# The last of four stages rewritten as one program, with rows kept on chip and weights loaded a stage earlier

## The chip, the cores and the metric

The kernel runs on one core of a Trainium2 chip, as one launch. The time is device microseconds (us) from the start of the program to its end; lower is better. Five engines of the core run their own instruction lists and meet through semaphores: TensorE (PE in the rows) multiplies matrices and transposes, VectorE (DVE) and ScalarE (ACT) do elementwise work and read PSUM, the memory that TensorE writes to; GpSimd (POOL) does small elementwise work, and SyncE (SP) only starts transfers here.

## The reference

Four layers run one after the other over 512 tokens of width 1024 in float32. The first three (attention with two softmaxes, attention in a neighbourhood, a gated delta rule) are not changed. The third leaves a residual stream `h` of 528 rows, 16 of them meta tokens. The fourth, cut to what matters:

```python
def shared_latent_kv(x, pos, g_norm, w_down, g_latent, w_uk, w_uv, k_gain):
    bsz, lp, _ = x.shape
    h = rms_norm_2(x, g_norm)
    c = h @ w_down
    c_kv = rms_norm_2(c[..., :KV_RANK], g_latent)
    k_pe = jnp.broadcast_to(c[..., None, KV_RANK:], (bsz, lp, MLA_HEADS, QK_ROPE))
    k_nope = (c_kv @ w_uk).reshape(bsz, lp, MLA_HEADS, QK_NOPE)
    v = (c_kv @ w_uv).reshape(bsz, lp, MLA_HEADS, V_HEAD)
    k = rms_norm_2(jnp.concatenate([k_nope, k_pe], -1), k_gain)
    k = jnp.concatenate([k[..., :QK_NOPE], rope(k[..., QK_NOPE:], pos)], -1)
    return k, v
...
def mla_layer(x, pos, k, v, g_norm, w_in, g_q_latent, w_uq, q_gain, w_out):
    bsz, lp, _ = x.shape
    h = rms_norm_2(x, g_norm)
    z = h @ w_in
    c_q = rms_norm_2(z[..., :Q_RANK], g_q_latent)
    gate = z[..., Q_RANK:]
    q = rms_norm_2((c_q @ w_uq).reshape(bsz, lp, MLA_HEADS, QK_DIM), q_gain)
    q = jnp.concatenate([q[..., :QK_NOPE], rope(q[..., QK_NOPE:], pos)], -1)
    o = chunk_causal_attention(q, k, v).reshape(bsz, lp, MLA_VW) * jax.nn.silu(gate)
    return x + o @ w_out
```

There are 8 heads; a query or key has 128 plain columns and 64 rotary ones, the rotary part of a key is the same for all heads, the latent of keys and values has 256 columns, that of queries 384, and the gate 1024.

## The kernel before

`program` (L3672) runs four stages. Tokens come in chunks: chunk 0 has the 16 meta rows, chunks 1 to 4 have 128 rows each. The third stage, `delta_layer` (L2910), ends with the output projection of its layer: TensorE (L2506), VectorE's add to the residual rows `d_rows` (L2860), and SyncE's store of each piece to `h3` in HBM (L2313). SyncE then waits until all stores have landed (L2314), and a barrier between blocks (L2915) holds all engines until it has.

The fourth stage is three functions, each a block of its own with a barrier behind it. Within a block each engine's order is the order of the code; a `Stages` object counts the named steps of an engine, and others wait for a name.

`latent_keys` (L2998): SyncE loads chunk after chunk of `h3` into two buffers in `m_tmp` (L3042), and between the second and the third chunk the gain columns, the identity, the rotary tables and `w_down` (L3046 to L3053), then the weights for keys and values (L3055) and for the query latent (L3057). For each chunk ScalarE squares and sums the row (L3081), GpSimd makes the reciprocal root (L3119, L3121), VectorE scales (L3162, one buffer `xn`), TensorE transposes 8 blocks (L3230), and VectorE (L3166) and then ScalarE (L3072) evacuate with the gains of keys and of queries. TensorE waits for all nine constants before its first transpose. Down projection `c` (L3251), its norm, its transposes (L3241). Then chunk by chunk: products for keys and values (L3269, 8 matmuls of 512 columns), squares (L3105), sums (L3203), root (L3136 to L3140), scaling (L3207), gain (L3211), rotary part (L3213), transposes (L3283, L3289), copies (L3098, L3196). The products of chunk t+1 stand ahead of the transposes of chunk t, and wait for the scaling of chunk t, since both use one pair of PSUM banks.

`latent_queries` (L3293): query latents (L3427), eight gate tiles (L3446, 8 matmuls of 512 columns each, tanh on ScalarE L3340, two steps on VectorE L3387 and L3389), then for each of four chunks of queries 9 matmuls of 512 columns (L3469), squares (L3349), sums (L3401), root (L3365, L3367), scaling (L3404), gain (L3408), rotary part (L3413 to L3417), transposes (L3481, L3486) and copies (L3345, L3395).

`latent_attention` (L3490): VectorE zeroes half of the two rotary buffers (L3597, L3599), ScalarE copies one half (L3572), and only then TensorE makes the first scores (L3525); 32 units of a head and a chunk, then the output projection (L3566), the add (L3625) and the stores.

A float32 matmul is two records in the trace (8 matmuls are x16), a transpose is one.

## Time and profile before

| | us |
|---|---|
| median of 3 runs | 3225.17 |
| lowest and highest | 3225.07, 3231.73 |
| the profiled execution, time | 3222.18 |
| its span | 3220.4 |

The profile is one execution, and its span begins and ends with the work on the engines; 1.8 us of the time lie around it. A row of the timeline gives start, duration, engine, line, what is written and read, and in brackets how long the engine had been idle and who ended that. A row of stretches gives the bounds and the length, then busy time with the number of instructions in brackets for PE, PEld (weight loads), DVE, ACT and POOL, then PEclk, the busy share of the DMA engines, and GB/s. A group of matmuls is shown some 0.16 us longer than it holds TensorE, because its last one is still draining when the next group starts; from one start to the next is the better length. The granted clock (PEclk) is a share of full speed: 1.00 is 2.4 GHz and 0.50 is 1.2 GHz.

### The profile page before, as it was taken

The page shows a single profiled execution, that of the slowest core. Times are in us where ns is not written, and L with a number is a line of the kernel's source. Part 1 is how long each engine was busy: PE and PEld are TensorE (multiplying, and loading weights), DVE is VectorE, ACT ScalarE, POOL GpSimd, SP SyncE. Part 2 cuts the span into 40 slices and gives each one's busy share as a digit, 9 for nine tenths or more (in the row PEclk, how much of TensorE's full clock was granted, in tenths as well). Part 3 has the DMA queues.
Part 4 walks back from the last instruction along what each step waited for, and adds up shares of the span by engine and source line. Part 5 has one row for each costly group of instructions (what it writes and reads, how often), then busy time and mean ns, then how long its engine had stood idle before and what let it go on. Part 6 is the DMA issues. An engine that isn't in the chain of part 4 may idle for free. (4 is left out here: it accounts for less than half of the span.)

```text
span 3220.4 us, 37627 instructions
## 1 busy us (share of the span) xinstructions
PE 3026.0 (94%) x14339; PEld 1959.2 (61%) x14339; DVE 1522.1 (47%) x3450; ACT 812.0 (25%) x2062; POOL 444.0 (14%) x745
## 2 busy tenths in 40 slices
PE   5999999999999997999999999979999999589699
PEld 2445555555555544887878786547888885244374
DVE  2344554554554435556556654334565563331431
ACT  1013333333333322123232332212122221120141
POOL 1221231231230010202011110000011110010000
PEclk8999999999999998999999999989999999799799
DMA  7330010010014004211212123042111100311001
GB/s 236 144 118 27 27 53 26 27 53 27 27 53 131 1 0 144 69 48 53 73 47 73 40 72 138 1 115 53 27 27 39 41 27 1 124 53 56 26 1 53
DMA packets 137899, 189.06 MB, mean 59 GB/s; under 512 B 21836, under 2 KB 90476, under 8 KB 135668
## 3 DMA queue, kind: packets, MB, share of 16 engines
q1 hardware_dynamic: 136520, 186.57, 18.2%
q8 instruction: 115, 1.88, 0.2%
q14 instruction: 64, 0.52, 0.1%
q10 hardware_dynamic: 1200, 0.09, 0.0%
HBM read 176.97 MB, written 9.67 MB: 58 GB/s over the span
## 5 line engine op out<-in xcount | busy, mean ns | idle before, releaser
L488 PE MATMUL a_psP<-a_w,a_uT 128*128 128x512 f32 x1536 | 700.1, 601 | 5.8 <-DMA a_w<-a_w_in 5.8
L488 PEld LDWEIGHTS a_psP<-a_w,a_uT 128*128 128x128 f32 x1536 | 280.5, 192 | 323.2 <-issue 323.2
L737 DVE TENSOR_REDUCE a_small<-a_psS 128x1 f32<-128x768 f32 (+1 forms) x192 | 140.8, 775 | 402.0 <-PE a_psS L516 402.0
L1460 PE MATMUL b_psP<-b_w,b_uT 128*128 128x256 f32 x768 | 183.8, 382 | 0.8 <-DVE b_raw L1743 0.3
L643 ACT ACTIVATE a_e<-a_psS,a_small 128x768 f32<-128x768 f32 (+1 forms) x192 | 143.8, 753 | 139.1 <-DVE a_small L737 138.7
L1460 PEld LDWEIGHTS b_psP<-b_w,b_uT 128*128 128x128 f32 x768 | 141.7, 190 | 23.7 <-issue 3.8
L1780 DVE TENSOR_REDUCE b_small<-b_psS 128x2 f32<-128x512 f32 x64 | 44.3, 691 | 213.0 <-PE b_psS L1517 213.0
L538 PEld LDWEIGHTS a_psO<-a_v,a_pT 128*128 128x128 f32 x896 | 115.1, 192 | 45.9 <-issue 45.9
L650 ACT COPY a_pT<-a_psS 128x768 f32<-128x768 f32 (+1 forms) x96 | 63.0, 656 | 311.4 <-PE a_psS L525 311.4
L1617 ACT ACTIVATE b_e<-b_psS,b_small 128x512 f32<-128x512 f32 x128 | 86.7, 682 | 192.0 <-DVE b_small L1793 190.1
L1624 ACT COPY b_e<-b_psS 128x512 f32<-128x512 f32 x128 | 71.8, 587 | 228.5 <-PE b_psS L1527 147.2
L2333 PE MATMUL d_ps<-d_uT,f_place 128*128 128x264 f32 x512 | 120.4, 388 | 6.4 <-DVE d_yT L2704 4.3
L1460 PE MATMUL b_psP<-b_wt,b_us 128*128 128x256 f32 x512 | 122.5, 387 | 4.1 <-DVE b_wt L1690 4.1
L2333 PE MATMUL d_ps<-d_uT,d_w 128*128 128x264 f32 x512 | 121.7, 392 | 4.8 <-DVE d_yT L2704 4.3
L516 PE MATMUL a_psS<-a_kT,a_qT 64*128 64x256 f32 (+1 forms) x640 | 122.4, 493 | 0.0
L538 PE MATMUL a_psO<-a_v,a_pT 128*128 128x128 f32 x896 | 115.5, 275 | 0.0
L1460 PEld LDWEIGHTS b_psP<-b_wt,b_us 128*128 128x128 f32 x512 | 96.1, 192 | 22.4 <-issue 6.6
L2333 PEld LDWEIGHTS d_ps<-d_uT,f_place 128*128 128x128 f32 x512 | 94.8, 190 | 24.2 <-DVE d_yT L2704 5.3
L2333 PEld LDWEIGHTS d_ps<-d_uT,d_w 128*128 128x128 f32 x512 | 95.9, 192 | 21.6 <-DVE d_yT L2704 5.3
L713 POOL TENSOR_TENSOR a_small<-a_small,a_eps_sum 128x1 f32<-128x1 f32 x96 | 18.2, 190 | 650.5 <-ACT a_dump L654 650.5
L800 DVE TENSOR_TENSOR a_work<-a_work 128x256 f32<-128x256 f32 x96 | 86.4, 939 | 0.4
L654 ACT ACTIVATE a_dump<-a_psO,a_small 128x128 f32<-128x128 f32 x96 | 35.3, 367 | 203.4 <-PE a_psO L538 203.4
(479 smaller groups left out, 5368.1 us busy)
## 6 DMA issues: line engine op xcount, KB each, us to landing
a_w<-a_w_in SPq DMA_DIRECT2D x16, 2048.0 KB, 8.7
b_w<-b_w_in SPq DMA_DIRECT2D x48, 512.0 KB, 3.8
a_yT<-mod_w SPq DMA_DIRECT2D x8, 1536.0 KB, 8.5
a_yT<-mod_w SPq DMA_DIRECT2D x8, 1024.0 KB, 18.2
b_yT<-b_w_in SPq DMA_DIRECT2D x16, 512.0 KB, 3.7
f_place<-bias_table SPq DMA_DIRECT2D x64, 128.0 KB
f_place<-a_w_in SPq DMA_DIRECT2D x16, 512.0 KB, 6.5
d_w<-a_w_in SPq DMA_DIRECT2D x16, 512.0 KB, 6.9
```

Source lines behind the costliest of these rows:

```text
L488: ins = nc.tensor.matmul(s.psP[:, x % 2, :], s.uT[:, a, t * P:(t + 1) * P], w[:, a, :], start=(a == 0), stop=(a == KD - 1))
L516: ins = nc.tensor.matmul(self.score_banks(k, keys)[:, a:b], s.qT[rows, h, t * P:(t + 1) * P], s.kT[rows, g % 2, h, keys.start + a:keys.sta ...
L538: ins = nc.tensor.matmul(s.psO[:, 0:P], s.pT[:, k * P:(k + 1) * P], s.v[:, g % 2, keys.start // P + k, h * P:(h + 1) * P], start=(k == 0), ...
L643: nc.scalar.activation(s.e[:, k, 0:n], self.score_banks(k, keys), ACT.Exp, bias=self.nm[i % 2][:, k:k + 1], accum_out=self.r[i % 4][:, k:k ...
L650: nc.scalar.copy(s.pT[:, 0:n], self.score_banks(0, keys)).then_inc(self.wTr, 1)
L737: nc.vector.tensor_reduce(self.nm[i % 2][:, k:k + 1], self.score_banks(k, keys), AX_X, ALU.max, negate=True).then_inc(self.mx, 1)
L800: nc.vector.tensor_tensor(r5[:, :, :, half, :], x5[:, :, :, 1 - half, :], sin, ALU.mult).then_inc(self.sined, 1)
L1460: ins = nc.tensor.matmul(out, lhsT, rhs, start=(a == 0), stop=(a == 3))
L1617: nc.scalar.activation(s.e[:, k, :].rearrange("p (b r c) -> p r b c", b=8, c=8), s.psS[:, k, :].rearrange("p (r b c) -> p r b c", b=8, c=8 ...
L1624: nc.scalar.copy(s.e[:, k, :], s.psS[:, k, :]).then_inc(self.wTr, 1)
L1780: nc.vector.tensor_reduce(self.m_ctx, ctx, mybir.AxisListType.XY, ALU.max).then_inc(self.cm, 1)
L2333: ins = nc.tensor.matmul(ps[:, 4, 0:n], s.w[h % 2][:, b, i, :], s.uT[:, b, half * n:(half + 1) * n], start=(b == 0), stop=(b == KD - 1))
```

## The change

The third stage's residual rows move to a buffer that lives through both stages (`Later.rows`, `g_rows`), and stage four reads them there. Weights and gain columns for keys are loaded by SyncE at the start of the third stage, behind its own loads (`Later.load`). The wait for the last stores moves out of the third stage to the first use that needs it (the first gate tile). The three functions of stage four become `LatentMixer` and `LatentAttention` in one block. Their PSUM banks are dealt so that keys (banks 0 to 3), queries (4 to 6) and gates (7) go side by side. The multiplication of keys and of the main part of queries by their gains moves into ScalarE's copies as a per-column scale; VectorE keeps the gain of the 64 rotary columns of queries. Two `xn` buffers take the place of one, and evacuation of a transposed chunk is split in halves between VectorE and ScalarE.

```diff
--- before.py
+++ after.py
@@ third stage
-        self.rows = sb("d_rows", [P, CH, D], F32)
+        self.rows = later.rows
...
         load_head(sp, s.w[1], a["a_w_in_2"][0], 1, self.w_in)
+        self.ahead(sp)
...
             sp.dma_start(self.h3[r, cols], s.rows[0:chunk_len(t), t, cols]).then_inc(self.stored, 16)
-        sp.wait_ge(self.stored, 16 * len(self.rest))
@@ loads at the start of the third stage
+    def load(self, sp, a, col_in, down_in, up_in):
+        g = self.gcol
+        for dst, src in ((g[:, 0:8], a["kv_norm_2"]), (g[:, 8:16], a["b_norm_2"][0]), (g[:, 16:18], a["kv_latent_norm_2"]),
+                         (g[:, 18:21], a["b_q_latent_norm_2"][0]), (g[:, 21:22], a["k_gain_2"][0:P]),
+                         (g[:, 22:23], a["b_q_gain_2"][0][0:P])):
+            sp.dma_start(dst, src.rearrange("(a p) -> p a", p=P), allow_slow_non_contiguous=True).then_inc(col_in, 16)
+        sp.dma_start(self.w_down[:, :].rearrange("p (a n) -> p a n", a=KD),
+                     a["kv_w_down_2"].rearrange("(a p) n -> p a n", p=P)).then_inc(down_in, 16)
+        w_u = self.w_u[:, :].rearrange("p (r a n) -> p r a n", r=2, a=2)
+        for r, name in enumerate(("kv_w_uk_2", "kv_w_uv_2")):
+            sp.dma_start(w_u[:, r], a[name].rearrange("(a p) n -> p a n", p=P)).then_inc(up_in, 16)
@@ LatentMixer, SyncE
+        sp.dma_start(s.w_cq, rows(W[:, 0:Q_RANK])).then_inc(self.cq_in, 16)
+        sp.dma_start(s.cos[:, :, :], a["rope2_cos"].rearrange("(t p) d -> p t d", p=P)).then_inc(self.rope_in, 16)
+        sp.dma_start(s.sin[:, :, :], a["rope2_sin"].rearrange("(t p) d -> p t d", p=P)).then_inc(self.rope_in, 16)
+        sp.dma_start(s.gain[:, 0, :], a["k_gain_2"][P:].partition_broadcast(P)).then_inc(self.rope_in, 16)
+        sp.dma_start(s.gain[:, 1, :], a["b_q_gain_2"][0][P:].partition_broadcast(P)).then_inc(self.rope_in, 16)
+        sp.dma_start(s.w_g[0], rows(W[:, Q_RANK:Q_RANK + BANK])).then_inc(self.g_in[0], 16)
+        sp.dma_start(s.w_uq, rows(a["b_w_uq_2"][0])).then_inc(self.uq_in, 16)
+        sp.wait_ge(te.sem, te.at("c%d" % LT))
+        sp.dma_start(s.w_g[1], rows(W[:, Q_RANK + BANK:Q_RANK + 2 * BANK])).then_inc(self.g_in[1], 16)
@@ LatentMixer, TensorE: the order, and the waits of a round
+        def gate(i):
...
+            elif i == 6:
+                aw("qT%d" % (LT - 1))
+            elif i == 7:
+                vw("sg5")
+            else:
+                vw("sg%d" % (i - 1))
...
+        def keys_values(t):
...
+            if t:
+                vw("kn%d" % (t - 1))
...
+                    if t and (r, j) == (0, 0):
+                        vw("kpT%d" % (t - 1))
...
+        def keys_T(t):
+            n = chunk_len(t)
+            vw("kp%d" % t)
...
+        def queries(t):
+            if t:
+                aw("qT%d" % (t - 1))
+                vw("qpT%d" % (t - 1))
...
+        for r in range(LT):
+            keys_values(r + 1)
+            gate(r + 1)
+            queries_T(r)
+            if r == LT - 1:
+                gate(5)
+            keys_T(r + 1)
+            if r < LT - 1:
+                queries(r + 1)
+        gate(6)
+        gate(7)
@@ LatentMixer, VectorE: a round
+        for r in range(LT):
+            key_sums(r + 1)
+            keys(r + 1)
+            gate(r + 1)
+            copy_qpT(r)
+            if r == LT - 1:
+                gate(5)
+            copy_kpT(r + 1)
+            if r < LT - 1:
+                query_sums(r + 1)
+                query_rest(r + 1)
+        gate(6)
+        gate(7)
@@ LatentAttention, VectorE: ahead of the first scores
+        dve.wait_ge(te.sem, te.at("kT%d" % LT))
+        nc.vector.memset(self.qp[1][0:64], 0.0).then_inc(self.qp_zero, 1)
+        dve.wait_ge(self.qp_odd, 1)
+        nc.vector.memset(s.qpT[64:128], 0.0).then_inc(self.qp_zero, 1)
@@ program
-                latent_keys(nc, sem, s, a, h3)
-                latent_queries(nc, sem, s, a)
-                latent_attention(nc, sem, s, a, h3, a["out"])
+                latent_layer(nc, sem, s, a, h3, a["out"], rows_stored, *ahead)
```

The order of TensorE in the queries of before, from the last gates to the third chunk of queries (`m_w2` and the gate weights print alike as `m_w`; L3469 are the query products, L3481 and L3486 their transposes):

```order
L3446 MATMUL m_ps<-m_w,m_ubT 128x512 x32
L3469 MATMUL m_ps<-m_w,m_cT 128x512 x18
L3481 MATMUL m_ps<-f_identity,m_tmp 128x128 x8
L3486 MATMUL m_ps<-f_identity,m_rot 128x128 x4
L3469 MATMUL m_ps<-m_w,m_cT 128x512 x9
L3481 MATMUL m_ps<-f_identity,m_tmp 128x128 x8
L3486 MATMUL m_ps<-f_identity,m_rot 128x128 x4
L3469 MATMUL m_ps<-m_w,m_cT 128x512 x9
```

The order of TensorE in one round of after (the products of keys and values L3202, one gate L3183, transposes of queries L3236 and L3240, of keys L3210 and L3214, products of queries L3229):

```order
L3202 MATMUL m_ps<-g_w_up,m_cT 128x512 x8
L3183 MATMUL m_ps<-f_place,m_ubT 128x512 x8
L3236 MATMUL m_ps<-f_identity,m_tmp 128x128 x8
L3240 MATMUL m_ps<-f_identity,g_rows 128x128 x4
L3210 MATMUL m_ps<-f_identity,m_tmp 128x128 x4
L3214 MATMUL m_ps<-f_identity,m_tmp 128x128 x8
L3229 MATMUL m_ps<-m_w,m_cqT 128x512 x9
```

Key products and a gate now stand between the products of a chunk of queries and its transposes, where before there were the products of the next chunk only, and two barriers lay between keys, queries and scores.

VectorE in the queries of before, one chunk (sums, scaling, copy of the chunk before, gain over 1536 columns, four rotary steps):

```order
L3401 TENSOR_REDUCE m_tiny<-m_tmp 128x8
L3404 TENSOR_TENSOR m_tmp<-m_ps,m_tiny 128x1536
L3395 COPY m_qpT<-m_ps 128x4x128
L3408 TENSOR_TENSOR m_tmp<-m_tmp,m_gain 128x1536
L3413 TENSOR_TENSOR m_rot<-m_tmp,m_sin 128x8x32
L3414 TENSOR_TENSOR m_rot<-m_tmp,m_sin 128x8x32
L3415 TENSOR_TENSOR m_rot<-m_tmp,m_cos 128x512
L3417 TENSOR_TENSOR m_rot<-m_rot 128x512
```

VectorE in a round of after, from the scaling of a chunk of queries on:

```order
L3518 TENSOR_TENSOR m_tmp<-m_ps,m_tiny 128x1536
L3520 TENSOR_TENSOR m_tmp<-m_tmp,m_gain 128x8x64
L3526 TENSOR_TENSOR g_rows<-m_tmp,m_sin 128x8x32
L3527 TENSOR_TENSOR g_rows<-m_tmp,m_sin 128x8x32
L3528 TENSOR_TENSOR g_rows<-m_tmp,m_cos 128x512
L3530 TENSOR_TENSOR g_rows<-g_rows 128x512
L3493 TENSOR_REDUCE m_tiny<-m_tmp 128x8
L3500 TENSOR_TENSOR m_tmp<-m_ps,m_tiny 128x1024
L3503 TENSOR_TENSOR m_tmp<-m_kpe,m_tiny 128x512
L3485 TENSOR_SCALAR g_w_down<-g_w_down 128x512
L3487 TENSOR_TENSOR g_rows<-g_w_down,m_ps 128x512
L3534 COPY g_w_down<-m_ps 128x4x128
```

The gain of queries is 512 columns (L3520) instead of 1536, the gain of keys is gone, and the sums and the scaling of keys (L3493, L3500, L3503) stand behind the whole of the queries' part and ahead of the gate (L3485, L3487) and of the copy (L3534).

SyncE at the start of the third stage of after, behind the first heads' weights (the last row is the third stage's own next load):

```order
L2239 DMA d_w<-a_w_in 128x8x128 x4
L2979 DMA g_columns<-kv_norm 128x8x1
L2979 DMA g_columns<-b_norm 128x8x1
L2979 DMA g_columns<-kv_latent_norm 128x2x1
L2979 DMA g_columns<-b_q_latent_norm 128x3x1
L2979 DMA g_columns<-k_gain 128x1
L2979 DMA g_columns<-b_q_gain 128x1
L2980 DMA g_w_down<-kv_w_down 128x8x320
L2984 DMA g_w_up<-kv_w_uk 128x2x1024
L2984 DMA g_w_up<-kv_w_uv 128x2x1024
L2239 DMA f_place<-a_w_in 128x8x128 x4
```

Nine loads, 3.3 MB, are new there; in before they stand in stage four, between the second and the third chunk of rows and behind the last chunk.

## Rows read from the trace of the kernel before

**Rows 1.** Timeline of the border between stages three and four, all engines.

```profile
2777.58 0.69 DVE L2860 TENSOR_TENSOR d_rows<-d_rows,d_ps 128x512 f32<-128x512 f32 x1 [1.03 <-PE d_ps L2506]
...
2780.78 0.07 DVE L3154 MEMSET m_half<- 128x8 f32 x1 [2.51 <-PEq L2915]
...
2782.67 1.05 ACT L3081 ACTIVATE m_v<-m_tmp 16x1024 f32<-16x1024 f32 x1 [36.89 <-DMA m_tmp<-h]
...
2784.80 0.74 DVE L3162 TENSOR_SCALAR m_tmp<-m_tmp,m_tiny 16x1024 f32<-16x1024 f32 x1 [3.59 <-POOL m_tiny L3121]
...
2794.64 1.03 PE L3230 MATMUL m_ps<-f_identity,m_tmp 16*128 16x16 f32 x8 [17.10 <-DMA m_sin<-rope_sin]
```

**Rows 2.** Busy time of each engine, granted clock and DMA in three stretches.

```profile
2778.00:2795.00 17.00, 0.35 (x4) 0.36 (x4) 1.41 (x5) 2.29 (x4) 1.46 (x4) 0.62 0.65 158
2795.00:2814.00 19.00, 8.28 (x39) 6.84 (x38) 10.34 (x36) 9.73 (x30) 2.21 (x6) 0.50 0.75 271
...
2981.00:3052.00 71.00, 43.06 (x121) 21.17 (x119) 36.05 (x36) 12.13 (x10) 7.36 (x8) 0.80 0.08 30
```

**Rows 3.** Timeline of TensorE: down projection, key transposes, query latents, gates, queries.

```profile
2828.88 4.47 PE L3251 MATMUL m_ps<-f_place,m_ukT 128*128 128x320 f32 x16
...
2867.98 1.04 PE L3283 MATMUL m_ps<-f_identity,m_tmp 128*128 128x128 f32 x8
2868.86 0.60 PE L3289 MATMUL m_ps<-f_identity,m_tmp 128*128 128x128 f32 x4
...
2895.44 20.88 PE L3427 MATMUL m_ps<-m_w,m_ubT 128*128 128x384 f32 x64 [1.05 <-PEq L3035]
...
2953.38 27.63 PE L3446 MATMUL m_ps<-m_w,m_ubT 128*128 128x512 f32 x64
2980.85 15.61 PE L3469 MATMUL m_ps<-m_w,m_cT 128*128 128x512 f32 x36
```

**Rows 4.** Timeline of one chunk of keys: squares, sums, scaling.

```profile
2864.75 1.02 ACT L3105 ACTIVATE m_tmp<-m_ps 128x1024 f32<-128x1024 f32 x1 [5.01 <-PE m_ps L3269]
...
2865.81 1.22 DVE L3203 TENSOR_REDUCE m_tiny<-m_tmp 128x8 f32<-128x1024 f32 x1 [3.00 <-ACT m_tmp L3105]
...
2869.34 1.22 DVE L3207 TENSOR_TENSOR m_tmp<-m_ps,m_tiny 128x1024 f32<-128x1024 f32 x1 [2.31 <-POOL m_tiny L3140]
```

**Rows 5.** Timeline of one chunk of queries: squares, sums, scaling, last rotary step.

```profile
2988.77 1.45 ACT L3349 ACTIVATE m_tmp<-m_ps 128x1536 f32<-128x1536 f32 x1 [7.13 <-PE m_ps L3469]
...
2990.26 1.75 DVE L3401 TENSOR_REDUCE m_tiny<-m_tmp 128x8 f32<-128x1536 f32 x1 [7.43 <-ACT m_tmp L3349]
...
2994.05 1.76 DVE L3404 TENSOR_TENSOR m_tmp<-m_ps,m_tiny 128x1536 f32<-128x1536 f32 x1 [2.04 <-POOL m_tiny L3367]
...
2999.03 0.69 DVE L3417 TENSOR_TENSOR m_rot<-m_rot 128x512 f32<-128x512 f32 x1
```

**Rows 6.** Timeline of one gate: tanh, then the product with it.

```profile
2974.18 0.60 ACT L3340 ACTIVATE m_rot<-m_ps 128x512 f32<-128x512 f32 x1 [6.27 <-PE m_ps L3446]
...
2975.27 0.69 DVE L3389 TENSOR_TENSOR m_sg<-m_rot,m_ps 128x512 f32<-128x512 f32 x1
```

**Rows 7.** Timeline ahead of the first scores.

```profile
3047.88 1.76 DVE L3597 MEMSET m_tmp<- 64x2048 f32 x1 [0.77 <-PEq L3316]
3050.13 1.76 DVE L3599 MEMSET m_qpT<- 64x2048 f32 x1 [0.48 <-issue]
...
3052.04 0.58 PE L3525 MATMUL m_ps<-m_kT,m_qT 128*128 128x16 f32 x2 [5.66 <-DVE m_qpT L3599]
```

**Rows 8.** Timeline of TensorE at the third stage's start, transposes only.

```profile
2149.11 3.68 PE L2067 MATMUL d_ps<-f_identity,d_cq 128*128 128x128 f32 x16 [1.12 <-DVE d_cq L2140]
2152.97 1.52 PE L2067 MATMUL d_ps<-f_identity,d_cq 128*128 128x128 f32 x8 [0.18 <-DVE d_cq L2140]
```

**Rows 9.** Timeline of SyncE: its first loads behind the third stage's start.

```profile
2197.62 4.18 SPq L2238 DMA_DIRECT2D f_place<-a_w_in  x4
```

**Rows 10.** Transfers of stage four: one load, its size and time from issue to landing.

```profile
m_w<-b_w_in SPq DMA_DIRECT2D x1, 1536.0 KB, 11.4
```

More of the change, by code:

```diff
@@ L2940, in _ @@
             mixer.vector(dve)
+    return mixer.stored, 16 * len(mixer.rest)
 def delta_masks():
@@ new lines, in __init__ @@
+        self.w_down = later.w_down[:, :].rearrange("p (a n) -> p a n", a=KD)
+        self.w_u = later.w_u[:, :].rearrange("p (r a n) -> p r a n", r=2, a=2)
+        self.w_cq = self.kT[:, :, :].rearrange("p h n -> p (h n)")[:, 0:KD * Q_RANK].rearrange("p (a n) -> p a n", a=KD)
+        self.w_uq = self.w2[:, :].rearrange("p (a n) -> p a n", a=3)
+        flat = self.ukT[:, :, :].rearrange("p a n -> p (a n)")[:, 0:KD * BANK]
+        self.w_g = [x.rearrange("p (a n) -> p a n", a=KD) for x in (front.place[:, :], flat)]
@@ new lines, in gate, with key_sums @@
+        def gate(i):
+            n, t = self.gates[i]
+            if i == 0:
+                dve.wait_ge(*self.rows_stored)
+            aw("tanh%d" % i)
+            ve.done(nc.vector.tensor_scalar(s.th, s.th, 0.5, 0.5, ALU.mult, ALU.add), "th%d" % i)
+            me("th%d" % i)
+            ve.done(nc.vector.tensor_tensor(s.sg[:, t, n * BANK:(n + 1) * BANK], s.th, ps[:, self.gate_bank(i), :], ALU.mult),
+                    "sg%d" % i)
+        def key_sums(t):
+            n = chunk_len(t)
+            aw("sqk%d" % t)
+            ve.done(nc.vector.reduce_sum(self.kss[t % 2][0:n], heads(s.tmp[0:n, 0, 0:D], P), AX_X), "ssk%d" % t)
@@ new lines, in copy_qpT @@
+        def copy_qpT(t):
+            tw("qpT%d" % t)
+            ve.done(nc.vector.tensor_copy(s.qpT[:, :, self.tok(t)], heads(ps[:, 6, :], P)), "qpT%d" % t)
+        nc.vector.memset(s.half[:, :], -0.5)
+        nc.vector.memset(s.kpe[:, 0], 0.0)
+        ve.done(nc.vector.memset(s.eps[:, :], EPS), "memsets")
+        normed(0)
+        normed(1)
+        scale_uk(0)
+        normed(2)
+        scale_uk(1)
+        normed(3)
+        scale_uk(2)
+        latent(0)
+        normed(4)
+        scale_uk(3)
@@ new lines, in vector @@
+        latent(1)
+        scale_uk(4)
+        for t in range(3):
+            scale_c(t)
+            latent(t + 2)
+        scale_c(3)
+        query_latent(0)
+        scale_c(4)
+        query_latent(1)
+        key_rotation()
+        query_latent(2)
+        query_latent(3)
+        for t in range(3):
+            scale_cq(t)
+        gate(0)
+        key_sums(0)
+        scale_cq(3)
+        keys(0)
+        query_sums(0)
+        copy_kpT(0)
+        query_rest(0)
+        for r in range(LT):
+            key_sums(r + 1)
+            keys(r + 1)
+            gate(r + 1)
+            copy_qpT(r)
+            if r == LT - 1:
+                gate(5)
+            copy_kpT(r + 1)
+            if r < LT - 1:
+                query_sums(r + 1)
+                query_rest(r + 1)
@@ L3328, in _ @@
+            attention.sync(sp)
+        @block.tensor
+        def _(pe):
+            mixer.tensor(pe)
+            attention.tensor(pe)
         @block.scalar
         def _(act):
[L3330 to L3335 removed]
@@ L3336, in _ @@
-            for i in range(2 * LT):
-                act.wait_ge(te.sem, te.at("z%d" % i))
-                if i >= 2:
-                    act.wait_ge(ve.sem, ve.at("sg%d" % (i - 2)))
-                ac.done(nc.scalar.activation(s.rot[:, i % 2, :], s.ps[:, 6 + i % 2, :], ACT.Tanh, scale=0.5), "tanh%d" % i)
-            def copy_q(t):
-                act.wait_ge(te.sem, te.at("qT%d" % t))
-                ps = s.ps[:, 4 * (t % 2):4 * (t % 2) + 2, :].rearrange("p b n -> p (b n)")
-                ac.done(nc.scalar.copy(s.qT[:, :, tok(t)], heads(ps, P)), "qT%d" % t)
@@ L3347, in _ @@
[L3347 to L3352 removed]
+            mixer.scalar(act)
+            attention.scalar(act)
         @block.gpsimd
         def _(pool):
[L3356 to L3361 removed]
@@ L3362, in _ @@
-            for t in range(LT):
-                pool.wait_ge(ve.sem, ve.at("ss%d" % t))
-                x = qrs[t % 2]
-                po.done(nc.gpsimd.tensor_tensor(x, qss[t % 2], s.eps[:, :], ALU.add), "qms%d" % t)
-                pool.wait_ge(po.sem, po.at("qms%d" % t))
-                po.done(nc.gpsimd.tensor_tensor(x, x, s.half[:, :], ALU.pow), "qrs%d" % t)
+            mixer.gpsimd(pool)
         @block.vector
         def _(dve):
-            me = lambda name: dve.wait_ge(ve.sem, ve.at(name))
@@ L3383, in _ @@
-            for i in range(2 * LT):
-                n, t = i // LT, i % LT
-                th = s.rot[:, i % 2, :]
-                dve.wait_ge(ac.sem, ac.at("tanh%d" % i))
-                ve.done(nc.vector.tensor_scalar(th, th, 0.5, 0.5, ALU.mult, ALU.add), "th%d" % i)
-                me("th%d" % i)
-                ve.done(nc.vector.tensor_tensor(s.sg[:, t, n * BANK:(n + 1) * BANK], th, s.ps[:, 6 + i % 2, :], ALU.mult),
-                        "sg%d" % i)
-            half = ROPE_W // 2
```

1140 lines of the change are left out of this document (573 added, 567 removed).

## Prediction

> **What bounds the kernel now.** The third stage ends with VectorE's add at 2777.58, over at 2778.27 [rows 1], and the first scores begin at 3052.04 [rows 7]. These 273.8 us are all that the change rewrites; what comes before and behind is the same work in the same order. I read the stretches first: the granted clock is 0.62, 0.50 and 0.80 in three of them [rows 2], so here TensorE is neither always busy nor at full speed. Then I counted what TensorE has to do here at full clock.
>
> **TensorE's work**, durations start to start where the next row allows it, else less the 0.16 us of drain that 27.63 shows over 27.47 [rows 3]. A 512-column matmul is two records of 0.429 us: 27.47/64. So a gate tile (16 records) is 6.87, keys and values of a chunk (16) 6.87, a chunk of queries (18) 7.73. A down projection is 4.31, the four query latents 20.7. Eight transposes are 0.88 (2867.98 to 2868.86), so 0.11 each [rows 3]. In sum: 5 down projections 21.6, latents 20.7, 8 gates 54.9, keys and values 5 x 6.87 = 34.3, queries 4 x 7.73 = 30.9, and some 160 transposes 17.6 (rows, keys, queries, latents; those of the 16-row chunk shorter). That is 180.0 us, before and after alike: no matmul goes or comes. Before loses 273.8 - 180.0 = 93.8 us to waits and to the low clock. The question is what after loses.
>
> **Part 1, the start.** Before: TensorE's first transpose is at 2794.64, 16.4 us behind the last add, held by the constants that queue behind rows on SyncE [rows 1], and then row transposes crawl from chunk to chunk at clock 0.50 [rows 2] until the first down projection.
> After: rows and gains lie on chip. The barrier opens without the landing of the stores. VectorE's first instruction stood 2.51 us behind its last [rows 1]; a barrier with no transfer to wait for cost VectorE 0.77 [rows 7], and SyncE's last issue ends a few tenths behind the add, so I take 0.75 for ScalarE's first square. Squares to scaled row took 2784.80 - 2782.67 = 2.13, the scaling 0.74 [rows 1]: first transposes at 0.75 + 2.13 + 0.74 = 3.6. ScalarE's squares follow each 1.16 (1.05 and the read of the sum), so the second scaled row is ready at 4.8. At the low clock eight transposes take 1.9; the third chunk's wait for VectorE, which first evacuates chunk 0, ends at 6.9, and the first down projection starts at 8.8.
> The clock: at the start of the third stage transposes alone ran from 2149.11, 3.68 us for 16, and the next 8 took 1.52, between the 1.9 of the low level and the 0.88 of the high one [rows 8]: it rose some 4.8 us after they had become dense. Dense from 4.8, after rises at about 9.9, so the first down projection pays another 0.55. By its end 6.6 us of work are done in 13.6: **7.0 lost**.
> The Trainium skill (TensorE: Matmul & The Clock Gate, Part 4: PE-mode transpose) says that the clock's high level does not engage for transposes, since they don't count as busy. By that rule only the down projection would begin to raise it, and the loss would be some 1.5 us more. The row decides otherwise: in it the clock rises in the middle of transposes, and I take the row.
>
> **Part 2, dense from there to round 0.** Down projections, latents, gate 0, keys 0, queries 0 follow each other. What hides the rest: each dense piece is 4.3 us or more, while the longest answer it waits for (squares 0.7, root 0.8, scaling 0.5) is 2 us and belongs to the piece before last. Loads: the latents' weights, 1.5 MB, took 11.4 us to land [rows 10] and are due 32 us into the stage; the gate's and the queries' (2.0 and 2.3 MB) are due at 54 and 69. With the rotary tables all this is 6.3 MB, 23 us at the 271 GB/s of [rows 2]. Lost: 0, unless the rate fell below 6.3/69, a third of that.
>
> **Part 3, the rounds.** Let T be where the products of chunk r+1 of keys start, right behind queries r. VectorE's chain: squares on ScalarE at T+0.2; sums 1.49 later; scaling 3.79 later (sums, GpSimd's root); its 1.76 and the gain, now 512 columns instead of 1536 (0.7 instead of 1.79); four rotary steps 2.1. Queries are ready at 0.2 + 1.49 + 3.79 + 1.79 + 0.7 + 2.1 = T+10.1 [rows 5]. Then the keys: sums to scaling 3.53 (2865.81 to 2869.34), scaling 1.14 in a row of instructions, rotary part 0.65: T+15.4 [rows 4]. TensorE has 6.87 + 6.87 (keys and values, gate), then transposes of queries 1.32: it is at the key transposes at T+15.05 and waits until 15.45. **0.4 lost.** It is done at 16.8. VectorE went on: the gate's tanh was there (T+13.74+0.8), the gate took 1.1 [rows 6], then the copy of the rotary queries 0.6: T+17.15, and queries r+1 need it. **0.4 lost.** A round is 24.1 of work and 24.9 long.
> The exceptions: in round 0 the transposes of keys 0 (1.32) stand between the end of queries 0 and T. The copy of rotary keys 0 comes behind the sums of queries 0, 0.2 + 1.49 + 1.75 + 0.6 = 4.05 after the queries' end or T+2.75, and the second half of the key products needs it at T+1.7: 1.1 lost, with the hand-over. The rest of its chain starts 1.3 earlier than in other rounds and has no wait. Rounds 1 and 2 lose 0.8 each. In round 3 gate 5 stands behind the query transposes and needs gate 4's bank free at T+16.6: 1.55. It then covers the key transposes. Sum: 1.1 + 0.8 + 0.8 + 1.55 = **4.3 lost**.
>
> **Part 4, the end.** Before, TensorE stood idle 5.66 ahead of the scores [rows 7]. After, the barrier is gone, but VectorE has the last gate ahead of the two halves' zeroing. From the end of gate 7: tanh 0.2 + 0.6, gate 0.04 + 1.15 [rows 6], then 3047.88 to 3052.04 = 4.16 as before [rows 7]: **6.1 lost**. A wait of the same length takes the place of the old one.
>
> **Part 5, nothing.** The nine loads in the third stage come behind the head's weights; SyncE's next load there is at 2197.62 [rows 9], over 40 us after the last of the old ones, and 3.3 MB take 12 us at 271 GB/s. Issuing them costs SyncE some 5 us of that. Attention and output projection have the same order; their weights are issued earlier than before. The gains moved into ScalarE's copies cost nothing there: it is busy 6 us in a round of 25. If that cover were gone, each copy would add its 1.0 to a round.
>
> **The sum.** After's stretch: 180.0 + 7.0 + 0 + 4.3 + 6.1 = 197.4. Before's: 273.8. Gain 76.4. The profiled execution goes from a span of 3220.4 to 3144.0; its time was 3222.18, 3 us under the median of 3225.17, and from the median I get 3225.2 - 76.4 = 3148.8, so **3149 us**.
>
> **Rivals.**
> 1. The chain of VectorE and GpSimd becomes the bound of the rounds. For: it ends 0.4 behind TensorE already, with nothing to spare, and every hand-over (ten in a round) was taken at its shortest. If the chain is 10% longer, 17.15 becomes 18.9, three rounds lose 1.7 more and round 3 as much: 7 us; and idles of some 2 us between short groups of transposes are what the stretch at clock 0.50 looks like [rows 2]; about 2 us lost at the low level in three rounds would be another 6. Against: the durations come from the same instructions. 3156 to 3163.
> 2. Transposes don't raise the clock at the start (the rule above, as a mechanism of this kernel): first down projection all at the low level, 3149 + 1.5 = 3150.5. Against: [rows 8].
> 3. The program doesn't run as dense as its text: transfers of 6.3 MB or the new barrier hold the start, up to the 16.4 us that TensorE waited before less the 3.6 I take: 3162. For: all loads share one queue. Against: nothing that TensorE needs in the first 32 us is among them.
> 4. Slower than before: the clock. If the denser stretch were held at the lower level, each microsecond of its 180 would take two; from 76.4/180 = 42% of the work at 0.50 the gain is gone, and all of it would give 3329. Against: the gates of before ran 27.5 us without a gap, all at 0.429 a record [rows 3], twice the columns per microsecond of the low level.
>
> **Chances.** Forecast 0.77, rival 1 0.14, rival 2 0.04, rival 3 0.04, rival 4 0.01. The unknown costs: at the low end the waits of the rounds vanish and the barrier costs 0.3 (-4.7, 3144); the zeroing or the gate may overlap a little more (-2). At the high end every hand-over of Part 3 is 0.15 longer (+6), and the range takes in rivals 1 and 3. Range 3142 to 3162. A measurement of this kernel can tell about 0.2% (6 us) from no change: faster 0.98, within it 0.01, slower 0.01.
>
> **What would show it.** First transposes 3.6 us behind the last add and the first down projection at 8.8; full clock from 10 on; rounds of 24.9 with two idles of 0.4 before the key transposes and the query products, released by VectorE; 1.5 before gate 5; 6.1 before the scores; the stretch 197. Wrong would be: an idle over 2 us in a round, a wait for a transfer, or a third stage longer than before.

## Result and profile after

The changed kernel takes 3145.36 us, the kernel before beside it 3225.12 (medians of four runs each; ratio 0.976, 95% interval 0.9743 to 0.9777). The forecast was 3149. Run twice more on other occasions it took 3148.59 beside 3221.52 and 3147.79 beside 3221.98 (ratios 0.9775 and 0.9769). The three gains are 79.8, 72.9 and 74.2, where 76.4 was forecast. Its profiled execution took 3144.98, with a span of 3143.2.

The table holds the stretch that was rewritten, from the last add of stage three to the first scores, and its neighbours, of before and of three profiles of the changed kernel:

| us | before | after | after, 2nd | after, 3rd |
|---|---|---|---|---|
| first transposes of stage three to last add | 634.4 | 636.1 | 634.2 | 631.2 |
| last add to first transposes | 16.4 | 3.7 | 3.7 | 3.7 |
| last add to first down projection | 35.9 | 8.6 | 8.9 | 8.9 |
| last add to first scores | 273.8 | 198.0 | 199.0 | 199.0 |
| first scores to the end of the span | 168.4 | 167.6 | 171.5 | 171.4 |

So the gain lies in the stretch: 75.8 us of 77.2 in the spans. The third stage's length differs by 5 us from run to run with the same kernel, so a cost of the nine loads in it would be seen only above that.

The start, which answers to [rows 1], in the timeline of the changed kernel (start, duration, engine, line, operation, idle before and who ended it; `...` stands for rows left out, here and below):

```profile
2776.96 0.69 DVE L2860 TENSOR_TENSOR g_rows<-g_rows,d_ps 128x512 f32<-128x512 f32 x1 [1.03 <-PE d_ps L2506]
...
2778.42 1.05 ACT L3292 ACTIVATE m_v<-g_rows 16x1024 f32<-16x1024 f32 x1 [34.36 <-PEq L2915]
2778.48 0.07 DVE L3536 MEMSET m_half<- 128x8 f32 x1 [0.82 <-PEq L2915]
...
2781.35 1.03 PE L3126 MATMUL m_ps<-f_identity,m_tmp 16*128 16x16 f32 x8 [4.42 <-DVE m_tmp L3427]
...
2782.82 3.47 PE L3126 MATMUL m_ps<-f_identity,m_tmp 128*128 128x128 f32 x16 [0.44 <-DVE m_tmp L3427]
...
2786.22 4.48 PE L3137 MATMUL m_ps<-g_w_down,m_ukT 128*16 128x320 f32 x16
2790.63 1.09 PE L3126 MATMUL m_ps<-f_identity,m_tmp 128*128 128x128 f32 x8
```

The add is over at 2777.65. VectorE is released 0.82 behind it, the first transposes come 3.70 behind it (forecast 3.6) and the first down projection 8.57 (8.8). That group takes 4.48, its length at full clock. The clock, in stretches, with the columns of [rows 2] (the granted clock is the third number from the end of a row):

```profile
2782.80:2785.50 2.70, 2.68 (x12) 2.46 (x13) 2.43 (x12) 0.99 (x5) 1.70 (x3) 0.50 1.16 333
2785.50:2786.50 1.00, 1.00 (x8) 0.66 (x7) 0.95 (x4) 0.98 (x4) 0.00 (x0) 0.82 1.29 249
2786.50:2788.00 1.50, 1.50 (x7) 0.58 (x6) 1.50 (x6) 1.50 (x5) 0.00 (x0) 1.00 0.98 350
2975.60:2995.60 20.00, 19.81 (x106) 15.15 (x106) 6.33 (x28) 6.57 (x25) 0.00 (x0) 0.88 0.00 1
2777.70:2975.60 197.90, 184.81 (x594) 96.05 (x595) 84.00 (x159) 52.09 (x102) 29.15 (x51) 0.98 0.19 66
```

From the end of stage three's matmuls at 2776.9 up to 2786.2 TensorE does nothing but transposes. The granted clock falls to 0.50 in the idle before them, and rises within the second of these stretches, at 2785.85. From the last add to the first scores it is 0.98. The last rounds and the end, TensorE's rows that answer to [rows 3, 5 and 7]:

```profile
2855.56 1.98 PE L3202 MATMUL m_ps<-g_w_up,m_cT 128*128 128x512 f32 x4
2858.25 5.42 PE L3202 MATMUL m_ps<-g_w_up,m_cT 128*128 128x512 f32 x12 [0.71 <-DVE m_kpT L3508]
...
2880.85 7.03 PE L3202 MATMUL m_ps<-g_w_up,m_cT 128*128 128x512 f32 x16
...
2896.24 0.66 PE L3210 MATMUL m_ps<-f_identity,m_tmp 128*128 128x128 f32 x4 [0.18 <-DVE m_tmp L3503]
...
2897.95 7.96 PE L3229 MATMUL m_ps<-m_w,m_cqT 128*128 128x512 f32 x18 [0.18 <-issue]
2905.75 7.03 PE L3202 MATMUL m_ps<-g_w_up,m_cT 128*128 128x512 f32 x16
...
2930.65 7.03 PE L3202 MATMUL m_ps<-g_w_up,m_cT 128*128 128x512 f32 x16
...
2945.25 0.60 PE L3240 MATMUL m_ps<-f_identity,g_rows 128*128 128x128 f32 x4
2947.09 7.13 PE L3183 MATMUL m_ps<-m_ukT,m_ubT 128*128 128x512 f32 x16 [1.24 <-DVE g_rows L3487]
...
2955.38 13.90 PE L3183 MATMUL m_ps<-m_ukT,m_ubT 128*128 128x512 f32 x32
2975.62 0.58 PE L3627 MATMUL m_ps<-m_kT,m_qT 128*128 128x16 f32 x2 [6.34 <-DVE g_w_down L3715]
```

From one start of key products (L3202) to the next is 24.90, twice. A round has two small idles, before the key transposes (L3210) and before the query products (L3229); 1.24 stand before gate 5 and 6.34 before the first scores.

### The profile page after: what moved, and what is told of

It reads as the page before. It is cut to its first block and busy times, and to the rows that moved or that the text cites. A ratio compares the mean times of both kernels' runs of the same rounds, so it can differ in the third digit from the quotient of the medians.

```text
span 3143.2 us, 37586 instructions
## 1 busy us (share of the span) xinstructions
PE 3009.9 (96%) x14339; PEld 1953.3 (62%) x14339; DVE 1512.0 (48%) x3445; ACT 814.4 (26%) x2062; POOL 446.5 (14%) x745
## 5 line engine op out<-in xcount | busy, mean ns | idle before, releaser
L2333 PEld LDWEIGHTS d_ps<-d_uT,d_w 128*128 128x128 f32 x512 | 95.8, 192 | 21.5 <-DVE d_yT L2704 5.3
```

The costliest lines, as they stand in the source:

```text
L2333: ins = nc.tensor.matmul(ps[:, 4, 0:n], s.w[h % 2][:, b, i, :], s.uT[:, b, half * n:(half + 1) * n], start=(b == 0), stop=(b == KD - 1))
```

## The experiments

The changed kernel was run again beside some of them, as a reference on the same chip.

> The changed kernel itself, as the same-chip reference for the three kernels beside it. Expected: its recorded median again, 3145.4 us, within 0.2%; last add of stage three to first score matmul about 198 us, of which the end (last gate to first scores) 6.5.

> The changed kernel as the same-chip reference for the two beside it. Expected: within 0.2% of 3147, ratio 0.9765; the first down projection at the start of the last stage takes 4.5 us when the clock has risen in the transposes and up to 5.3 when it has not yet.

Measured: 3148.59 and 3147.79; the table above has their stretches. The first down projection took 5.3 in both, against 4.48 in the first profile: the clock rose later. Differences of times below are against 3148.59 for e1, e3 and e6, and against 3147.79 for e8 and e9. For e2, e4, e5 and e7 only the kernel before ran beside them, so they are taken against 0.9772 times its time, 3147.6. Differences of the stretch are against 198.0 and 199.0, the shortest and the longest in the table, or against 199.0 alone.

**The start, undone in parts.** First the loads only, which go back to the head of stage four:

```diff
 third stage, SyncE:
-        self.ahead(sp)
 stage four, SyncE:
+        s.later.load(sp, a, self.col_in, self.down_in, self.up_in)
```

> The nine loads of gain columns and of the weights of keys go back to the head of the last stage's list on SyncE; the rows still stay on chip. Theory (SyncE issues the first three strided loads in 1.7 us each, and these and the down projection's weights now land behind the first transposes, but the start of the changed kernel is mainly rows on chip and no store to wait for): VectorE waits for the columns until some 9 us behind the last add instead of 6, the first down projection comes at 13 to 14 instead of 8.6, the rest is unchanged: total 4 to 7 us more than the changed kernel, near 3151. Rival (taking the loads out of the start is most of what the start gained): 12 us or more.

Measured: 3148.28, 1 us more, within what can be told apart, where 4 to 7 was expected; the stretch 201.4, 2.4 to 3.4 more. In the timeline of this kernel:

```profile
2782.92 1.23 DVE L3437 TENSOR_SCALAR m_ukT<-m_ps,g_columns 128x16 f32<-128x16 f32 x8 [1.32 <-DMA g_columns<-b_q_gain]
...
2784.86 1.97 PE L3127 MATMUL m_ps<-f_identity,m_tmp 128*128 128x128 f32 x8 [1.24 <-DVE m_tmp L3428]
...
2786.88 6.17 PE L3138 MATMUL m_ps<-g_w_down,m_ukT 128*16 128x320 f32 x16
```

VectorE's wait of 1.32 for a gain column ends 6.4 behind the add (over at 2776.50), where some 9 was expected, and the down projection comes at 10.4, not at 13 to 14. The expectation took 1.7 us for the issue of each of the first three columns, as in the third stage; here they took 0.38 to 0.67. So the direction was right and the size was half or less. TensorE never waits for the weights. Then the rows only, read back from HBM:

```diff
+        sp.wait_ge(*self.rows_stored)
+        for t in range(CH):
+            sp.dma_start(s.h[0:chunk_len(t), t, :], self.h3[chunk_cols(t), :]).then_inc(self.h_in[t], 16)
```

> The rows are read back from HBM, as in the kernel before, five loads on SyncE once the stores have landed; the nine loads stay in stage three. Theory (the store's landing and the reload stand on the path to the first square, each some 2 to 3 us): first transposes 9 us behind the last add instead of 3.7, then as in the changed kernel: total 5.5 us more, 4 to 7. Rival (the reload is most of the start's gain, because the chunks come one by one and the clock stays low among them): 12 us or more. Rival 2 (the queue is free by then and the rows come as fast as VectorE finishes): under 2 us.

Measured: 3153.33, 5.7 more as expected, though not by the path expected. The first transposes come 7.0 behind the add instead of the 9 that the theory gave, and the chunks that follow wait for their rows too; the down projection comes at 12.7 and the stretch is 203.2, which is 4.2 to 5.2 more. Rows and loads together explain some 8 of the 25 us that the start gained, by their traces. The order of the chunks is the third part (several lines are written as one in this cut):

```diff
-        x_T(0); x_T(1); x_T(2); down(0); x_T(3); down(1); x_T(4)
+        x_T(0); x_T(1); x_T(2); x_T(3); x_T(4); down(0); down(1)
 VectorE:
-        normed(0); normed(1); scale_uk(0); normed(2); scale_uk(1); ...
+        for t in range(CH):
+            normed(t)
+            scale_uk(t)
 ScalarE, before each half of its evacuation:
+                act.wait_ge(ve.sem, ve.at("ukT%d" % t))
```

> Only the start's order is undone: a chunk's rows are scaled when the chunk before has been evacuated by VectorE, ScalarE evacuates behind VectorE instead of each taking half, and all five row transposes stand ahead of the first down projection. Rows, loads and the rest are as in the changed kernel. Theory (that order, and not the transfers, was most of the start's loss: a chunk took 4.88 us in the kernel before, with 2.91 us of idle that keeps the clock at the lower level): first transposes 3.7 us behind the last add as before, four chunks of 4.88, the first down projection 23 us behind the add instead of 8.6 and at the low level; total 14 us more than the changed kernel, 12 to 17, near 3161. Rival (the transfers and constants made the start long, and with the rows on chip the chunks follow each other quickly whatever the order): less than 4 us more.

Measured: 3160.74, 12.9 more than the changed kernel beside it (3147.79), the stretch 211.4 against 199.0. TensorE's rows in this kernel:

```profile
2777.44 1.03 PE L3126 MATMUL m_ps<-f_identity,m_tmp 16*128 16x16 f32 x8 [4.42 <-DVE m_tmp L3424]
2780.45 1.97 PE L3126 MATMUL m_ps<-f_identity,m_tmp 128*128 128x128 f32 x8 [1.98 <-DVE m_tmp L3424]
2785.34 1.97 PE L3126 MATMUL m_ps<-f_identity,m_tmp 128*128 128x128 f32 x8 [2.91 <-DVE m_tmp L3424]
...
2797.00 9.44 PE L3137 MATMUL m_ps<-g_w_down,m_ukT 128*16 128x320 f32 x32
```

Here are the 4.88 a chunk and the 2.91 of idle of the kernel before, with every row on chip and no transfer waited for. So the order is half of the start, by the trace 12.4 of 25. All three with the old order of loads:

> The whole start as in the kernel before, the rest as in the changed kernel: rows read back from HBM once stored, the loads of constants and weights among them in the old order, TensorE's first transpose behind the gain columns, the down projection's weights and the rotary tables, and the chunks one by one as in e8. Theory (the parts add up to the 25 us that the traces of the two kernels show for the start: 13 until the first transposes, which come 16.4 us behind the last add instead of 3.7, and the rest from the order of the chunks): total 25 us more than the changed kernel, 22 to 29, near 3172. Rival (the start was not worth that much, and the gain came from the rounds): 15 us or less.

Measured: 3169.24, 21.5 more, just under the 22 to 29 expected; by the traces the stretch is 224.4 against 199.0, 25.3 more. The two differ because the scores and what follows are 4.0 shorter in e9's profile than in the one beside it (167.5 against 171.4), with a granted clock of 0.88 and not 0.68 in their first 20 us. The first transposes and the first down projection stand 16.1 and 35.6 behind the add (before: 16.4 and 35.9):

```profile
2789.27 1.00 PE L3135 MATMUL m_ps<-f_identity,m_tmp 16*128 16x16 f32 x8 [16.83 <-DMA m_gain<-b_q_gain]
...
2808.79 10.06 PE L3146 MATMUL m_ps<-g_w_down,m_ukT 128*16 128x320 f32 x32
```

That is the start of before inside the changed kernel, and its price in the stretch is the 25 us. The three trials of one part each add up to some 20 by their traces. The rest goes with TensorE's wait for all constants, which only e9 has: its first idle, 16.83, is ended by the load of the rotary gain. That wait was not tried by itself.

The other 50 of the 75.8 us lie behind the first down projection, in keys, gates and queries. No run undoes all of them; the next two each undo a part of the interleaving. The two barriers were not put back by themselves. The one idle named after them ahead of the query latents is 1.05 [rows 3].

**The rounds.** Gates 1 to 7 taken out of them:

```diff
             keys_values(r + 1)
-            gate(r + 1)
             queries_T(r)
-            if r == LT - 1:
-                gate(5)
             keys_T(r + 1)
...
-        gate(6)
-        gate(7)
+        for i in range(1, 8):
+            gate(i)
```

> Gates 1 to 7 leave the rounds and stand in a row behind them (their outputs alternate between two banks, so that they run without a gap); keys and queries still alternate. Theory (a round is as long as the chain over VectorE and GpSimd, 24.5 us, and the gate of 6.9 us is work for TensorE inside it that costs nothing): a round stays near 24.5 without its gate, with idles of about 2 us before the rotary transposes of the queries and 4.4 before the transposes of the keys, and the seven gates then cost 48 us in a row: total about 25 us more than the changed kernel, near 3173, up to 33 more if the granted clock falls in those idles. Rival (the gain of the changed kernel comes from its start alone, or the chain is shorter than I think): rounds near 18 us, total less than 5 us more.

Measured: 3180.83, 33 more, the most that the expectation allowed; the stretch 234.2, 35 to 36 more. One of its rounds, and the clock behind its longer idle:

```profile
2881.33 7.03 PE L3202 MATMUL m_ps<-g_w_up,m_cT 128*128 128x512 f32 x16
...
2891.45 0.66 PE L3240 MATMUL m_ps<-f_identity,g_rows 128*128 128x128 f32 x4 [1.75 <-DVE g_rows L3524]
2896.71 1.11 PE L3210 MATMUL m_ps<-f_identity,m_tmp 128*128 128x128 f32 x4 [4.60 <-DVE m_tmp L3497]
2897.61 1.91 PE L3214 MATMUL m_ps<-f_identity,m_tmp 128*128 128x128 f32 x8
2899.32 9.48 PE L3229 MATMUL m_ps<-m_w,m_cqT 128*128 128x512 f32 x18
2908.64 7.03 PE L3202 MATMUL m_ps<-g_w_up,m_cT 128*128 128x512 f32 x16
```

```profile
2899.00:2901.50 2.50, 2.50 (x6) 1.33 (x5) 0.00 (x0) 1.11 (x1) 0.00 (x0) 0.50 0.00 0
```

A round is 27.31 with 6.87 less work in it than one of 24.90. The idles of 1.75 and 4.60 are where the theory put them. After the longer one the clock is 0.50, the eight transposes take 1.91 instead of 1.04 and the query products 9.48 instead of 7.96, some 2.8 us in a round: 24.5 + 2.8 is what is seen. So the gate inside a round is free, and more: in rounds with it the query products keep their 7.96. The rival (rounds of 18) falls.

All keys, then all queries, a gate still in each chunk while they last:

```diff
-        queries(0)
+        gate(1)
         keys_T(0)
         for r in range(LT):
             keys_values(r + 1)
-            gate(r + 1)
-            queries_T(r)
-            ...
+            if r < 2:
+                gate(r + 2)
             keys_T(r + 1)
-            ...
+        for r in range(LT):
+            queries(r)
+            gate(r + 4)
+            queries_T(r)
```

> All keys first, then all queries; the gates still fill in, one a chunk (gate 1 in keys 0, gates 2 and 3 in keys 1 and 2, none in keys 3 and 4, gates 4 to 7 in queries 0 to 3). The rest is the changed kernel. Theory (queries need more cover than one gate, since their chain of 10.1 us and the copy behind it are longer than 6.9, and only the alternation with the keys gives it): about 3.6 us lost in each of three query rounds, which are 19.5 us long, 3.5 in each of the two chunks of keys without a gate, and some 5 at the end, 25 in all against 10.8 in the changed kernel: total about 14 us more, near 3160, up to 25 more if the clock falls. Rival (a gate in each chunk is enough cover, the alternation adds nothing to it): within 4 us of the changed kernel.

Measured: 3174.44, 27 more, 2 over what the expectation allowed if the clock fell; the stretch 223.7, 25 more. The longest of its query rounds and the start of the next:

```profile
2934.24 10.51 PE L3225 MATMUL m_ps<-m_w,m_cqT 128*128 128x512 f32 x18 [0.83 <-issue]
...
2954.71 0.66 PE L3236 MATMUL m_ps<-f_identity,g_rows 128*128 128x128 f32 x4 [1.75 <-DVE g_rows L3522]
2956.42 9.66 PE L3225 MATMUL m_ps<-m_w,m_cqT 128*128 128x512 f32 x18 [1.05 <-issue]
```

From 2934.24 to 2956.42 are 22.2, where 19.5 was expected (the other two query rounds are 20.6 and 21.3). The idles of 1.75 and 1.05 stand where the theory put them, and what is missing is again the clock, with 10.51 and 9.66 for query products that take 7.96 elsewhere. The keys with a gate ran at 15.0 to 15.2 a chunk without a wait, those without a gate waited 3.06 each. A gate is enough cover for keys and not for queries. The rival falls.

**How near VectorE is to its edge.** The gain multiplications back on VectorE. (The expectation names GpSimd; in the changed kernel they are part of ScalarE's copies, as the edit shows.)

```diff
-ac.done(nc.scalar.mul(s.kT[...], ..., s.gcol[:, 21:22]), "kT%d" % t)
+ac.done(nc.scalar.copy(s.kT[...], ...), "kT%d" % t)
 VectorE, keys(t), behind the scaling:
+            ve.done(nc.vector.tensor_tensor(..., s.gain[0:n, 0:1, 0:P]..., ALU.mult), "kg%d" % t)
 and for queries, 192 columns of a head in place of 64:
-ve.done(nc.vector.tensor_tensor(tm[:, :, P:], tm[:, :, P:], ..., ALU.mult), "qg%d" % t)
+ve.done(nc.vector.tensor_tensor(tm, tm, ..., ALU.mult), "qg%d" % t)
```

> The gain multiplications of keys and queries go back from GpSimd to VectorE; nothing else. Theory (a round of 24.9 us is TensorE's own 24.2 plus two small waits, and the chain sums, scaling, gain, transposes, copy is at its edge, so what is added to it comes out as waits): the two waits in a round grow from about 0.34 each to some 2.7 in all, rounds 24.9 to about 27.2, total about 8 us more than the changed kernel, near 3153, more if the granted clock falls after the longer waits. Rival (VectorE is busy for only 11.6 of the 24.9 us of a round, so there is room): rounds stay at 24.9, total within 1 us of the changed kernel.

Measured: 3160.36, 11.8 more, where about 8 and more with a fallen clock was expected; the stretch 208.3, 9.3 more. TensorE in rounds 1 and 2, and the clock behind the two idles:

```profile
2884.60 7.03 PE L3202 MATMUL m_ps<-g_w_up,m_cT 128*128 128x512 f32 x16
...
2902.31 1.00 PE L3210 MATMUL m_ps<-f_identity,m_tmp 128*128 128x128 f32 x4 [2.50 <-DVE m_tmp L3505]
2903.11 1.91 PE L3214 MATMUL m_ps<-f_identity,m_tmp 128*128 128x128 f32 x8
...
2913.08 7.03 PE L3202 MATMUL m_ps<-g_w_up,m_cT 128*128 128x512 f32 x16
...
2930.78 0.66 PE L3210 MATMUL m_ps<-f_identity,m_tmp 128*128 128x128 f32 x4 [2.50 <-DVE m_tmp L3505]
2931.28 1.04 PE L3214 MATMUL m_ps<-f_identity,m_tmp 128*128 128x128 f32 x8
...
2940.29 7.03 PE L3202 MATMUL m_ps<-g_w_up,m_cT 128*128 128x512 f32 x16
```

```profile
2902.30:2905.00 2.70, 2.69 (x13) 2.69 (x14) 2.18 (x4) 0.00 (x0) 0.00 (x0) 0.53 0.00 0
...
2930.80:2932.50 1.70, 1.52 (x13) 1.31 (x13) 1.67 (x4) 0.15 (x1) 0.00 (x0) 1.00 1.03 400
```

Round 2 is 27.21, the theory's 27.2. Round 1 is 28.48: behind the same idle of 2.50 the clock fell there and not in the other. VectorE's busy time in a round rose from 11.43 to 13.73, and these 2.3 us came out as 2.3 us of wait in round 2 and before gate 5. In round 0, where its chain had room, only 1.0 came out. So VectorE is idle for about half of a round, and still what is added to its chain at the edge is added to the kernel. The rival falls.

**What is left to gain.** The zeroing of the rotary halves ahead of gates 6 and 7:

```diff
+        nc.vector.memset(self.qp1[0:64], 0.0).then_inc(self.qp_zero, 1)
+        dve.wait_ge(self.qp_odd, 1)
+        nc.vector.memset(s.qpT[64:128], 0.0).then_inc(self.qp_zero, 1)
         gate(6)
         gate(7)
```

> Only one thing differs from the changed kernel: the zeroing of the rotary halves and the copies that follow it are issued on VectorE and ScalarE ahead of gates 6 and 7, so that they no longer stand behind the last tanh. Theory (the idle 6.34 us before the first scores is the tail VectorE work alone, and VectorE has the time for it during the 13.9 us gates): the idle goes to under 0.5 us, the first scores run at full clock instead of the lower level, total about 7 us less than the changed kernel, near 3138. Rival (something else ends that wait, such as the last gate rows themselves, or VectorE takes the time back in the gates): under 2 us less, 3143 or more, with another instruction named before the first scores.

Measured: 3139.09, 9.5 less than the changed kernel beside it (3148.59). TensorE's last gates and first scores:

```profile
2959.44 13.90 PE L3185 MATMUL m_ps<-m_ukT,m_ubT 128*128 128x512 f32 x32
2973.18 0.29 PE L3635 MATMUL m_ps<-m_kT,m_qT 128*128 128x16 f32 x2
```

The idle is gone, the stretch is 191.5 (7.5 less, where 7 was expected), and the scores begin at 0.29 for a pair that took 0.58. The 9.5 us are more than the idle of 6.5. The first 20 us of the scores, in the changed kernel's second profile and in e1:

```profile
2975.30:2995.30 20.00, 19.79 (x83) 14.65 (x84) 4.93 (x22) 5.48 (x20) 0.00 (x0) 0.68 0.00 1
```

```profile
2973.20:2993.20 20.00, 18.78 (x117) 14.23 (x116) 8.45 (x33) 7.76 (x29) 0.00 (x0) 1.00 0.00 1
```

A mean clock of 0.68 over 20 us is 12.8 us at the lower level and 6.4 lost; in the first profile it was 0.88, or 2.4 lost. These 4.0 are the 3.9 by which the last parts differ in the table. In e1 the clock is 1.00, but the part from the first scores to the end is 166.4, against 167.6 and 171.5: 1.2 and 5.0 less. At full clock TensorE comes to an idle of 1.04 early in the scores, where it waits for ScalarE, so about 1.2 of what the clock gives is not kept.

The same with four moves in the orders of VectorE and TensorE (cut; the early zeroing of e1 is in it too):

```diff
 VectorE:
             ve.done(..., "qn%d" % t)
+            key_sums(t + 1)
             me("qn%d" % t)
...
         keys(0)
-        query_sums(0)
         copy_kpT(0)
+        query_sums(0)
...
             keys(r + 1)
-            gate(r + 1)
             copy_qpT(r)
+            gate(r + 1)
 TensorE:
             queries_T(r)
-            if r == LT - 1:
-                gate(5)
             keys_T(r + 1)
+        gate(5)
```

> The early zeroing and, besides, four moves in the order in which VectorE and TensorE get the work of a round: the sums of the next keys between a query's scaling and its gain, the copy of the rotary query ahead of the gate, the first copy of the rotary key ahead of the first query sums, and gate 5 after the transposes of the last keys. Theory (each remaining wait is a place in VectorE's order, not a lack of time): 7 us for the end, 1.0 for the waits of the three rounds, 0.9 for round 0, 1.2 before gate 5, together about 10 us less than the changed kernel, near 3135, with rounds of 24.2 to 24.6. Rival (VectorE and GpSimd carry as much as they can, and a wait taken out here comes back there): the gain is the end's 7 us alone, or less, and rounds stay at 24.9.

Measured: 3135.55, 13.0 less than the changed kernel and 0.9735 of the kernel before (0.9722 to 0.9748): it is faster than both. Against e1 it is 3.5 less, where about 3 was expected, about what can be told apart; the trace is clearer. The stretch is 189.1, 2.4 less than e1's, though its start lost 1.0 more (the clock rose later). TensorE's starts of key products, and gate 5:

```profile
2860.30 7.13 PE L3203 MATMUL m_ps<-g_w_up,m_cT 128*128 128x512 f32 x16
...
2884.49 7.03 PE L3203 MATMUL m_ps<-g_w_up,m_cT 128*128 128x512 f32 x16
...
2908.57 7.03 PE L3203 MATMUL m_ps<-g_w_up,m_cT 128*128 128x512 f32 x16
...
2949.70 20.87 PE L3184 MATMUL m_ps<-m_ukT,m_ubT 128*128 128x512 f32 x48 [0.53 <-DVE g_rows L3488]
2970.40 0.29 PE L3631 MATMUL m_ps<-m_kT,m_qT 128*128 128x16 f32 x2
```

Rounds of 24.08 show no idle: TensorE's own work and nothing else. The rival (what is taken out here comes back there) falls.

## Why the prediction was right

The forecast rested on one count: what TensorE has to do in the stretch, and what keeps it from doing it. Each term came out within 1 us or so, so the total is right by its mechanism and not only by its sum. By its steps, the profile of the changed kernel against the working:

- **Work of 180.0.** e6 shows no idle but those of the start (7.5 lost) and 0.7 before gate 5, in a stretch of 189.1: 181 of work. Right to one.
- **Start, 7.0 lost.** The transposes of chunk 3 start 13.0 behind the add in the first profile and 14.0 in the second, against 13.6: 6.4 and 7.4 lost. Full clock came 8.2 behind the add in the first profile and 10.5 and 10.6 in the others, where 9.9 was forecast. (By the working's own 4.8 of [rows 8] it is 9.6; the slip is worth 0.15.) In the first profile the clock rose before there was any matmul in the stretch, and at the start of the third stage it rose among transposes too. The Trainium skill (TensorE: Matmul & The Clock Gate, Part 4: PE-mode transpose) states that the full clock does not engage for transposes; the trace does not agree, and the prediction was right to take the row. Rival 2 would have given the first down projection 8.6, twice its length; it took 4.48, and 5.3 in the others. The prediction priced that rival at 1.5, but 8.6 is 3.8 more than the 4.31 + 0.55 that it forecast for this group. e8 and e9 give the old start its old price.
- **Dense part, 0.** The trace has no idle from there to round 0, as forecast.
- **Rounds, 4.3 lost.** Against e6's 24.19 and 24.08, round 0 lost 1.1 (forecast 1.1), rounds 1 and 2 lost 0.82 each (0.8), and gate 5 came 1.40 late (1.55): 4.1. Both places and releasers are those named: VectorE each time, the row before the query products, given to "issue", included: it is gone in e6, which inside the rounds moves only VectorE's copy and sums.
- **End, 6.1 lost.** From 2955.38 the 32 records last 13.74 (32 times 0.429), so the idle begins at 2969.12 and is 6.5.
- **Part 5, nothing.** A third stage longer than before was named as a sign of being wrong, and in the first profile it is 1.7 longer (636.1 against 634.4), in the others 0.2 and 3.2 shorter: within its own scatter. e4 and e9 have no loads of weights in it, and it is 634.2 and 631.2 long, against 631.2 to 636.1 with them. The nine loads kept SyncE busy for 8.3 us, not 5, but its next load came 53.6 behind the stage's first transposes, before 53.8. So no cost is seen, within 5 us. The gains in ScalarE's copies show no wait either, and e3 shows what they saved.

The sum of the losses is 17 with 181 of work: 198.0 against 197.4. That the first median lies 4 us under the forecast is not in this stretch; the two later ones lie within 1.2 us of it.

The rivals: 1 (VectorE's chain becomes the bound) did not happen, but e3 shows how near it was. It added 2.3 us to the chain, and 2.3 us of wait came out in rounds 1 and 2 and before gate 5, with the clock on top in round 1. 3 (transfers hold the start) did not, and e4 shows that there was room for some of them. 4 (the dense stretch is held at the lower clock) did not: it was 0.98. 2 is answered under the start.

**What the working left out** is the price of the lower clock behind an idle. It counted the end as 6.1 on both sides, which was enough for the difference between the two kernels, since both idle there (5.66 and 6.34). But the lower clock behind the idle costs 2.4 to 6.4 in the scores, of which e1 got back 1.2 to 5.0. These 4 us and the 5 us of the third stage are the two differences seen between profiles of the changed kernel; where the third stage's come from stays open. The expectations for e2 and e7 had the same term outside their sums, only as a limit if the clock fell; it was some 2.8 us a round.

## What to carry to other kernels

Count the bounding engine's own work in a stretch at full clock and subtract it: what remains has to be put down to named waits, and a rewrite can then be forecast wait by wait. A fill-in tile between a long chain of answers and the instruction that needs them is worth the time that it covers and the clock that the idle would have cost (e2). In the rounds here the place of one instruction in VectorE's order (sums, a copy, a zeroing) set the wait, and not how busy VectorE was (e1, e6). At a stage's border ask for the order of the chunks as well as for the transfers: here each was about half.
